# A fused attention, convolution and expert-mixture kernel: ring buffers handed over by half chunks, and the first routing round split into two halves of eight experts

## What is computed

```python
def peer_ffn(hn, w_q, subkeys, u_tab, v_tab):
    ...
        q = (xc @ w_q).reshape(PEER_TOKEN_CHUNK, PEER_HEADS, 2, PEER_D_HALF)
        s = jnp.einsum('thcd,hcnd->thcn', q, subkeys, preferred_element_type=jnp.float32)
        s_top, i_top = lax.top_k(s, PEER_TOPK)
        cand = s_top[:, :, 0, :, None] + s_top[:, :, 1, None, :]
        cand_idx = i_top[:, :, 0, :, None] * PEER_N_KEYS + i_top[:, :, 1, None, :]
        best, pos = lax.top_k(cand.reshape(PEER_TOKEN_CHUNK, PEER_HEADS, PEER_TOPK * PEER_TOPK), PEER_TOPK)
        idx = jnp.take_along_axis(cand_idx.reshape(PEER_TOKEN_CHUNK, PEER_HEADS, PEER_TOPK * PEER_TOPK), pos, axis=-1)
        g = jax.nn.softmax(best, axis=-1)
        u = u_tab[idx]
        act = jax.nn.gelu(jnp.einsum('td,thkd->thk', xc, u), approximate=False)
        v = v_tab[idx]
        return jnp.einsum('thk,thkd->td', (g * act).astype(v_tab.dtype), v)
```

## Time and profile before

| | |
|---|---|
| median of three runs | 1514.26 us (1512.84 to 1515.54) |
| profiled execution | 1513.23 us, of which the span of the instructions is 1511.4 us |
| VectorE busy | 1088.9 us (72%) |
| TensorE matmul busy | 1038.8 us (69%), weight load 515.5 us (34%) |
| ScalarE busy | 615.2 us (41%) |
| POOL busy | 580.1 us (38%) |
| DMA | 603.29 MB, mean 399 GB/s over the span |
| of this the 512 gathers | 536.90 MB, 86.3% of the 16 engines' span |

### The profile page before, as it was taken

The page is one execution under the profiler, slowest core; times in us unless marked ns, Lnnn a source line. Parts: engine busy times, 40 slices in busy tenths (PEclk is TensorE's granted clock), DMA queues, the critical chain, the costliest instruction groups (busy, mean ns, idle before and its releaser), DMA issues.

```text
span 1511.4 us, 20941 instructions
## 1 busy us (share of the span) xinstructions
PE 1038.8 (69%) x6816; PEld 515.5 (34%) x6816; DVE 1088.9 (72%) x2934; ACT 615.2 (41%) x1856; POOL 580.1 (38%) x516
## 2 busy tenths in 40 slices
PE   9999876777756777666778777665777554444543
PEld 5645432322433454332334455332244211010100
DVE  5448668777645799998746788698786676666784
ACT  2324555553423446554244535354344433233321
POOL 0013444443333454543433434344334444444441
PEclk9999986567777788787887788578888755555555
DMA  9639999999999999999999999999999999999996
GB/s 388 242 137 398 419 419 419 418 413 413 416 420 419 420 397 419 418 415 397 418 420 420 402 417 414 420 415 397 412 407 417 417 419 420 419 420 419 420 418 268
DMA packets 82649, 603.29 MB, mean 399 GB/s; under 512 B 9734, under 2 KB 10502, under 8 KB 12012
## 3 DMA queue, kind: packets, MB, share of 16 engines
q0 software_dynamic: 73728, 536.90, 86.3%
q1 hardware_dynamic: 7852, 64.74, 10.5%
q10 hardware_dynamic: 960, 0.31, 0.1%
HBM read 600.87 MB, written 1.05 MB: 398 GB/s over the span
## 4 chain that ended last, share of the span: by engine, by line
DMA 39%; PE 21%; DVE 20%; issue 13%; ACT 6%; POOL 1%; SPq 0%; DVEq 0%; POOLq 0%; ACTq 0%
DMA ring<-table_dram,idx 37%; PE bank L637 8%; DVE ring L1695 8%; PE ypsum L637 6%; PE qpsum L637 4%; ACT L1104 2%; DVE arena L1578 2%; PE spsum L637 1%; POOL ring L630 1%; DMA arena<-c_out_dram 1%; ACT wts L1104 1%; DVE topi L1627 1%; ACT gel L1104 1%; DMA ring<-w_in_dram 1%; DVE eq L1628 1%
## 5 line engine op out<-in xcount | busy, mean ns | idle before, releaser
L630 POOL DMA_INDIRECT ring<-table_dram,idx x512 | 579.9, 1133 | 909.2 <-PE ypsum L637 540.4
L1695 DVE CUSTOM_DVE_ANT_0 ring<-xns,ring 128x1024 f32<-128x1024 f32 x512 | 623.3, 1223 | 295.5 <-DMA ring<-table_dram,idx 292.3
L637 PE MATMUL ypsum<-ring,wts 128*32 128x256 f32 x4096 | 425.3, 504 | 428.5 <-ACT wts L1104 427.7
L1104 ACT ACTIVATE gel<-dot 128x1 f32<-128x1 f32 x512 | 103.2, 202 | 714.9 <-DVE dot L1695 713.4
L637 PEld LDWEIGHTS ypsum<-ring,wts 128*32 128x32 f32 x4096 | 96.0, 124 | 681.5 <-ACT wts L1104 624.3
L1104 ACT ACTIVATE wts<-gident,gel 128x32 f32<-128x32 f32 x512 | 164.6, 321 | 17.4
L1104 ACT ACT_TABLE_LOAD x83 | 106.5, 1283 | 5.2 <-issue 3.8
L637 PE MATMUL qpsum<-arena,hT 128*128 128x256 f32 (+1 forms) x416 | 99.5, 414 | 2.4 <-ACT hT L1104 2.4
L1578 DVE SCALAR_TENSOR_TENSOR arena<-arena,cols 128x128 f32<-128x128 f32 x300 | 88.5, 346 | 0.6
L637 PE MATMUL qpsum<-arena 128*128 128x128 f32 x372 | 83.7, 361 | 0.0
L637 PEld LDWEIGHTS qpsum<-arena,hT 128*128 128x128 f32 (+1 forms) x416 | 71.9, 193 | 26.1 <-issue 12.9
(11 more groups left out here) (194 smaller groups left out, 1018.3 us busy)
## 6 DMA issues: line engine op xcount, KB each, us to landing
arena<-heads_dram SPq DMA_DIRECT2D x12, 1152.0 KB, 9.8
head<-heads_dram SPq DMA_DIRECT2D x8, 1152.0 KB, 10.1
ring<-table_dram,idx POOLq DMA_INDIRECT x512, 13.2
arena<-c_in_dram SPq DMA_DIRECT2D x4, 2048.0 KB, 19.1
ring<-w_in_dram SPq DMA_DIRECT2D x3, 2048.0 KB, 18.1
arena<-c_out_dram SPq DMA_DIRECT2D x6, 1024.0 KB, 9.0
arena<-w_out_dram SPq DMA_DIRECT2D x1, 4096.0 KB, 37.2
arena<-heads_dram SPq DMA_DIRECT2D x1, 3456.0 KB, 16.4
```

What stands on the lines that cost most here:

```text
L630: pool.indirect_dma_start(out=row(b), out_offset=None, in_=table[:, :], in_offset=bass.IndirectOffsetOnAxis(ap=idx[R % 2][:, k:k + 1], axi ...
L637: return nc.tensor.matmul(o_, l, r, start=start, stop=stop, **kw)
L1104: return nc.scalar.activation(out_, in_, func, **kw)
L1695: V.tensor_tensor_reduce(out=u, in0=xnr[G % 2], in1=u, scale=1.0, scalar=0.0, op0=ALU.mult, op1=ALU.add, accum_out=dot[:, k:k + 1]).then_i ...
```

## The change

There are four edits, all at the start of the expert work.

1. Half chunks. In `project(1, c)`, for the four chunks of 512 columns, the matmul of the fourth of eight contraction blocks raises a new semaphore, `win_half_used`. POOL waits for it before slots 0, 2, 4 and 6, and for the whole chunk before slots 1, 3 and 5.
2. The product of tile 1 with chunk 0 leaves its place before the slot loop. TensorE makes its first half after `add_slot(0)` and its second half after `add_slot(1)`. The early work of round 1 moves one slot back: `early_queries(1)` from s == 0 to 1, `early_turn(1)` from 1 to 2, `early_scores_of(1)` from 2 to 3. ScalarE takes the product at s == 1, after `weigh_slot(1)`.
3. The first routing. A new function `first_route` takes the place of `route(0, 2)` to `route(0, 5)`. It looks up the best eight and writes their index columns before it searches for the next eight. The first write raises `half_routed`, the second `routed`.
4. POOL waits for `half_routed` at slot 0 and for `routed` at slot 8.

```diff
@@ POOL @@
             for n in range(ALL_SLOTS):
                 R, k = divmod(n, TOPK)
                 b = n % RING
-                if k == 0:
+                if n == 0:
+                    pool.wait_ge(half_routed, 1)
+                elif n == TOPK // 2:
+                    pool.wait_ge(routed, 1)
+                elif k == 0:
                     pool.wait_ge(routed, R + 1)
                 if n < RING:
-                    c = WIN_AT.index(n // 2)
                     if n % 2 == 0:
-                        full(pool, PROJ_JOB[1][c])
+                        pool.wait_ge(win_half_used, n // 2 + 1)
+                    else:
+                        full(pool, PROJ_JOB[1][WIN_AT.index(n // 2)])
                 pool.wait_ge(ring_free, n + 1)
@@ TensorE @@
                     last = mm(bank[:, 0:w], hTs[t][:, k, :], win_[c][:, k, :], k == 0, k == KD - 1)
+                    if t == 1 and w == CHUNK and k == KD // 2 - 1:
+                        last.then_inc(win_half_used, 1)
...
             def beside_attention(s):
-                if s == 0:
+                if s < 2:
+                    project(1, 0, range(s * KD // 2, (s + 1) * KD // 2))
+                if s == 1:
                     for H in range(QUAD):
                         pe.wait_ge(first_in[H], first_parts[H] * 16)
                     early_queries(1)
-                if s == 1:
+                if s == 2:
                     early_turn(1)
-                if s == 2:
+                if s == 3:
                     early_scores_of(1)
...
             project(1, 1)
             project(1, 3)
-            project(1, 0)
@@ VectorE @@
+            def first_route():
...
+                own.then(V.tensor_tensor(cand.rearrange("p (a b) -> p a b", a=TOPK),
+                                         top_[:, 0, :].unsqueeze(2).to_broadcast([P, TOPK, TOPK]),
+                                         top_[:, 1, :].unsqueeze(1).to_broadcast([P, TOPK, TOPK]), ALU.add))
+                for half in range(2):
+                    k = slice(half * m, (half + 1) * m)
+                    from_ = sc if half else cand
+                    settle(dve)
+                    own.then(V.max(best[:, k], from_))
+                    settle(dve)
+                    own.then(V.max_index(pos[:, k], best[:, k], from_))
+                    own.did(V.tensor_scalar(pos2_[:, 0, k], pos[:, k], 4, None, ALU.logical_shift_right))
+                    own.then(V.tensor_scalar(pos2_[:, 1, k], pos[:, k], TOPK - 1, None, ALU.bitwise_and))
+                    for c in range(2):
...
+                        own.did(V.tensor_tensor(eq_, pos2_[:, c, k].unsqueeze(2).to_broadcast([P, m, TOPK]),
+                                                iota16[:, :].unsqueeze(1).to_broadcast([P, m, TOPK]), ALU.is_equal))
+                    for c in range(2):
...
+                        own.wait(1)
+                        own.did(V.tensor_tensor(eq_, eq_, topf_[:, c, :].unsqueeze(1).to_broadcast([P, m, TOPK]), ALU.mult))
+                    for c in range(2):
...
+                        own.wait(1)
+                        own.did(V.tensor_reduce(sel_[:, c, k], eq_, AX.X, ALU.add))
+                    own.wait()
+                    V.scalar_tensor_tensor(out=idx[0][:, k], in0=sel_[:, 0, k], scalar=float(KEYS), in1=sel_[:, 1, k],
+                                           op0=ALU.mult, op1=ALU.add).then_inc(routed if half else half_routed, 1)
+                    if half == 0:
+                        own.then(V.match_replace(sc, best[:, k], cand, -3.0e38))
+                V.tensor_scalar(nbest[:, :], best[:, 0:1], -1.0, None, ALU.mult).then_inc(best_ready, 1)
...
             first_start()
-            for part_ in range(6):
+            for part_ in range(2):
                 route(0, part_)
+            first_route()
             gates(0, 0)
```

12 lines of the change are left out of this document (11 added, 1 removed).

## The result

The changed kernel took 1516.18 us (median of 16 runs, 1514.84 to 1518.51), the kernel before 1514.08 (16 runs, 1511.98 to 1515.54). The ratio is 1.0015, with a 95% interval of 1.0008 to 1.0022: slower by 2.3 us, between 1.2 and 3.3. The profiled execution has a span of 1514.3 us against 1511.4.

What follows compares the result with a forecast made beforehand. The kernel was taken as a DMA-bound queue of 512 gathers: stream start, bytes and holes. Terms -1.65, +1.55 and +2.1 gave +2.0 us: 1515.2 like the profiled execution, 1516.3 against the median; range 1511.9 to 1518.1.

Steps and rivals of the forecast that it cites:

- The first index: VectorE's first routing: eight small operations and a short write put the first gather 2.3 us sooner, issued at 103.55.
- Half chunks: POOL's slots 1 to 5: each issued with over 4 us of backlog, none starves, the stream runs 2.3 us ahead.
- Slots 6 to 9: Gathers around the moved product: slot 6 at 120.0, slot 9 at 129.1; lead 1.65 us at slot 8, then about 1.6 lost.
- old hole: The kernel before, after slot 6: DMA at 298 GB/s from 122.9 to 128.4 us, a loss of 1.6 us.
- the faster rival: The early start is kept: slots 6 to 8, issued sooner, may also close the 1.6 us hole; chance 0.17.
- VectorE's lateness: VectorE behind the moved product: latents at 123.85, 2.25 us later; round 1's routing at 131.2, 3.3 us late, as is slot 16.
- The hole at slot 16: Gather of slot 16, issued at 149.2 with 1.15 us backlog: stream loses 2.1 us, between bounds of 0.1 and 3.3.
- Sum: Stream at slot 8 -1.65, hole at slot 9 +1.55, hole at slot 16 +2.1: together +2.0 us, kept to the end.
- The dips: Sign of being right: DMA rate below 350 GB/s for some us near 122, 131 and 151.
- The early start is kept: Holes at slots 9 and 16 don't open, stream stays 1.65 to 2.3 us ahead or more: 1510.2 to 1512.6; chance 0.17.
- A short backlog costs nothing: A gather need only be issued before the one ahead ends: slot 16 loses 0.1, whole +0.1, 1514.4; chance 0.18.
- VectorE's full lateness: Lower rate persists at slots 17 and 18: +3.3 us or a little more, 1517.6; chance 0.22.

Runs made afterwards that it cites:

- move_halves: The changed kernel without the split first routing: half chunks and the moved product, all sixteen indices written at once; +3.3 us (1.8 to 4.8) against the kernel before.
- halves_route: The changed kernel without the moved product: half chunks and split first routing, chunk 0 whole before the slot loop; -0.8 us (-2.1 to +0.6) against the kernel before.
- dots_weights_first: As dots_first, and ScalarE writes the weights of slots 2 and 3 ahead of its takes; -1.5 us (-2.9 to -0.3) against the kernel before.
- adds_first_1: As dots_weights_first, latents behind slot 4's dots, chunk 0's first half before the slot loop, `add_slot(1)` ahead of `early_queries(1)`, early work at old slots; 1511.73 us, -2.7 us.
- halves_dots_first: halves_route with VectorE's dots of slots 3 and 4 before the latents, 5 and 6 before round 1's routing; -0.9 us (-2.3 to +0.3) against the kernel before.
- route_only: The split first routing alone, with whole chunks and the product in its old place; -0.3 us (-1.5 to +1.1) against the kernel before.
- vector_late_2: The kernel before with two idle VectorE operations behind the latents of tile 1; slot 16 is 0.8 us late, no timed difference given.
- before_again: The kernel before profiled once more, no edit, not timed beside it; from the index search to the end 0.8 us longer.
- dots_first: The changed kernel with VectorE's dots of slots 3 to 5 before the latents, slot 6 before round 1's routing; +0.3 us (-1.1 to +1.5) against the kernel before.
- vector_late_5: The kernel before with five idle VectorE operations (2.27 us) behind the latents of tile 1; 0.0 us (-1.5 to +1.7) against the kernel before.
- move_only: The moved product alone, with whole chunks and all sixteen indices written at once; 7.6 us slower (5.6 to 9.5) than the kernel before.
- adds_first_2: As adds_first_1, with `add_slot(2)` also ahead of the early queries; -0.9 us (-2.3 to +0.6) against the kernel before.

## Why the prediction was right

The forecast was +2.0 us, measured are +2.3 (1.2 to 3.3), and 2.2 on the stream at 71 in the profile. The mechanism was right at slot 16 and in kind at slot 9; that the sum came so close is in part luck, since errors of 1.1 and 1.6 us at slots 6 to 9 stood against each other. By its own steps:

- **The first index**: right. I took 2.3 us sooner; it is 2.46, the upper end. The eight operations take 1.60 us behind the search (102.07 to 103.67), 0.20 each. That half of the 0.26 could be exposed latency was a guess that no run tests. The Trainium skill, "VectorE: DVE Perf Modes", section on the TRN2 errata, has a formula by which an operation of 128 elements takes 0.29 us (an estimate from it); the trace does not agree for such a run, and the measurement decides.
- **Half chunks**: right. Slots 3 to 5 are issued 3.43 us apart, as the halves end, and none starves: the lead at 15 is 2.4 us.
- **Slots 6 to 9**: the places are right, the stream's course between them is not. Slot 6 was put at 120.0 and slot 9 at 129.1; less the 1.43 us of the execution they are at 120.33 and 129.71. Each addition costs the product 0.57 us and not 0.45 (116.65 to 117.22). (The terms given for `add_slot(2)` sum to 127.4 and not to 127.6; it came at 128.2.) The sum had the lead fall to 1.65 at slot 8 and kept the whole old hole. In fact slots 6 to 8, issued 1.3, 1.2 and 3.7 us sooner than before, closed part of that hole, as the faster rival had said: the lead was 2.7 us at slot 9's issue. But then slot 9 had 0.4 us of work ahead of it and not 2.1, and 3.1 us were lost there and not 1.55. Together the two places lost 2.8 us, where the sum had 0.65 + 1.55 = 2.2.
- **VectorE's lateness**: right in kind, a sixth too small. The sum put the latents at 123.85, and they are at 124.51. It put the routing 3.3 us late, and it is 3.97; slot 16 is as late to a hundredth (3.96). The 0.66 us that the product took longer than forecast stand again in the routing's start; the 1.05 us that the sum added behind the latents are there (3.97 - 2.91). move_halves has this lateness without the split routing. halves_route, without the move, starts its latents in time (121.31, 21.41 from the index search); its 1.9 us come from ScalarE's pause behind them. So it is the move that makes VectorE late.
- **The hole at slot 16**: I took 2.1 us between bounds of 0.1 and 3.3; it measured 1.8 (0.4 at 38 to 2.2 at 71). The lower bound took 1.4 us from an issue to the data. The traces have 1.8: up to 107.60 nothing is moved after the first issue at 105.84.
- **Sum**: -2.3 + 2.2 + 2.1 = +2.0 by the forecast (its -1.65 at slot 8 holds the first 0.65); -2.4 + 2.8 + 1.8 = +2.2 by the trace. The dips stand where they were put: 200 GB/s from 122.5 to 125.0 in the changed kernel's trace, 139 from 130.6 to 133.6, and 295 here:

```profile
149.62:151.62 2.00, 2.00 (x15) 1.24 (x15) 1.90 (x9) 1.56 (x5) 0.31 (x1) 1.00 0.76 295
```

The rivals. *The early start is kept* fell for the change as it is; but it needed only that VectorE be no more than about 1.3 us late, and dots_weights_first and adds_first_1 meet that (slot 16 0.3 and 1.2 us sooner) and keep 1.2 and 1.6 us. *A short backlog costs nothing* fell in six kernels. For each the table has the work ahead of slot 16 when it is issued, counted as in the prediction, by a window from the first issue to that one. The changed kernel's is

```profile
104.81:151.31 46.50, 41.71 (x266) 20.63 (x265) 30.14 (x100) 17.31 (x49) 17.98 (x16) 1.00 0.89 346
```

which is 16.09 MB of 16.78, so 1.6 us are left. Beside it stands what the stream lost from 38 to 46 and from 46 to 56 us from the index search. In the six kernels that lose anything slot 16 is issued between 47.3 and 51.3, so the first of the two losses lies ahead of it.

```
kernel               ahead of slot 16   lost 38 to 46   lost 46 to 56
halves_dots_first      5.4                0.0             0.0
the kernel before      4.55               0               0
route_only             4.4               -0.1             0.0
vector_late_2          4.3               -0.1             0.0
adds_first_1           4.2                0.0             0.0
before_again           3.8                0.0             0.0
dots_weights_first     3.7               -0.1             0.0
dots_first             3.0                0.6             0.6
vector_late_5          2.9                0.8             0.6
move_halves            1.9                0.8             1.4
the change             1.6                0.2             1.4
halves_route           1.5                0.0             1.4
move_only              1.2                0.1             1.6
```

By the rival, 1.4 us of work ahead would be enough, or 1.8 by the delay that the traces show. (adds_first_2 is left out: its hole opens ahead of slot 16.) Nothing is lost with 3.7 us or more ahead of slot 16; 0.6 us is lost near it with 3.0 and 2.9, and 1.4 to 1.6 with 1.9 and less. The loss from 38 to 46 is not slot 16's: in dots_first, vector_late_5 and move_halves earlier slots were short of work as well (slot 11 had 2.4, 2.5 and 3.2 us ahead of it, against 6.7 before). That bears on the Trainium skill's "DMA: Bandwidth & Descriptors", section on the anatomy of one DMA, by which the fixed 2.0 us of a DMA are mostly completion and little of it setup. The trace does not agree for these gathers of 1.05 MB: with an idle queue 1.8 us pass from the start of the first issue to its data, and a gather issued with 3.0 us of work ahead of it no longer keeps the stream full. Why 3.0 us is not enough where the delay is 1.8, no run shows. *VectorE's full lateness* (3.3 us or more lost) fell too: 4.0 us late cost 1.8, since the work queued ahead took up the first part.

In vector_late_5 the lateness was put in by hand, with no move and no split: 2.2 us of it cost the stream 1.4. That VectorE's dots are the link is thus shown from both sides, by adding lateness and, in dots_first, by taking it away. It is shown in the profiles' windows. In the timed runs dots_first shows it too, while the effect of vector_late_5 is below what they resolve.

Still open: why four of five executions of move_only took 3.3 to 5.6 us more than the profiled one, and what held ScalarE for 2.02 us in halves_route and for about 1.6 in move_only.

## What to carry to other kernels

When a queue of transfers bounds a kernel, count for each issue how much work is still ahead of it, and follow a moved piece of work through every engine that is ordered behind it: here a sooner first gather was worth 2.4 us, and the product moved behind two sums took back more in two places, at slot 9 by way of TensorE's late third sum and at slot 16 by way of VectorE's dots. If an in-order engine must wait for something that has become late, put in front of that wait whatever is ready and frees buffers. And place by a clock that starts at an unchanged instruction near the change: executions differed by up to 2.3 us at that instruction, as much as the effect.

## What the hardware showed that I had not expected

- The start of the expert work varies from one execution to the next: the first index search stands between 99.33 and 101.62 in 14 profiles. In the one at 101.62 TensorE waited 1.95 us for a weight load near 15 us (1.07 in the kernel before), and its granted clock, which before stays at 1.00 there, fell behind that. Windows of the changed kernel (the last but two columns are the granted clock, the DMA share and the rate):

```profile
15.00:17.00 2.00, 0.11 (x1) 0.00 (x0) 1.82 (x9) 0.69 (x1) 0.00 (x0) 1.00 0.97 401
17.00:18.00 1.00, 0.94 (x2) 0.49 (x3) 0.83 (x6) 0.00 (x0) 0.00 (x0) 1.00 1.16 492
18.00:19.00 1.00, 1.00 (x3) 0.53 (x2) 0.86 (x5) 0.00 (x0) 0.00 (x0) 0.66 0.88 377
19.00:20.00 1.00, 1.00 (x2) 0.34 (x1) 0.90 (x5) 0.00 (x0) 0.00 (x0) 0.50 1.11 475
20.00:30.00 10.00, 10.00 (x28) 4.73 (x27) 7.52 (x36) 3.99 (x11) 0.00 (x0) 0.91 0.99 416
```

  TensorE stood nearly idle for 2 us (0.11 busy) and ran at 0.50, the lower of its two levels (1.2 GHz), from about 18.3 to about 21.7.
- A wait can have no visible cause: 2.02 us on ScalarE, "remote", in halves_route, and it cost that profile its lead. move_only has one of about 1.6 us on ScalarE, and halves_dots_first one of 1.10 us on POOL ahead of slot 10. The other eleven profiles show none between 105 and 150 us.
- VectorE's multiplication by a constant of 512 elements, in place, takes 0.45 us (2.27 for five), not the 0.69 us of the two-input comparison and product of that size in the kernel before.
